# A two-layer transformer with a bidirectional RWKV block: recurrence tiles held by direction, with the two chunks on the two partition halves

## Time and profile before

| | |
|---|---|
| median of 3 runs | 1791.7 us (1791.41 to 1792.92) |
| time of the profiled execution | 1792.95 us |
| its span in the trace | 1791.0 us |
| mean granted TensorE clock | 0.943 of full speed |
| TensorE matmul busy | 1618.8 us (90%) |
| VectorE busy | 764.7 us (43%) |
| ScalarE busy | 376.5 us (21%) |
| DMA | 386.37 MB, mean 216 GB/s |

### The profile page before, as it was taken

How to read it: one execution, slowest core, us unless ns; L and a number is a source line. 1 busy time by engine, 2 the same in 40 slices (tenths; PEclk the granted TensorE clock), 3 DMA queues, 4 the chain that set the end, 5 groups by cost and what they waited for, 6 DMA issues and landing times.

```text
span 1791.0 us, 26168 instructions
## 1 busy us (share of the span) xinstructions
PE 1618.8 (90%) x10862; PEld 1098.8 (61%) x10862; DVE 764.7 (43%) x1562; ACT 376.5 (21%) x959; POOL 2.1 (0%) x6
## 2 busy tenths in 40 slices
PE   8999999999999999999999999999999766666666
PEld 5877878884587787888558778898854101102011
DVE  3476566665538755766555583131422000000001
ACT  4262131110416312211022641111211000000001
POOL 0000000000000000000000000000000000000000
PEclk9999999999999999999999999999999877768777
DMA  9324334535542332544534231111688999999997
GB/s 390 119 72 165 117 134 189 188 149 190 212 152 84 118 143 93 193 177 170 187 144 163 73 142 73 49 50 73 280 322 333 421 420 420 421 421 421 421 421 320
DMA packets 55521, 386.37 MB, mean 216 GB/s; under 512 B 6256, under 2 KB 6768, under 8 KB 10480
## 3 DMA queue, kind: packets, MB, share of 16 engines
q1 hardware_dynamic: 53424, 375.16, 53.2%
q10 hardware_dynamic: 1984, 9.57, 1.4%
HBM read 383.65 MB, written 1.05 MB: 215 GB/s over the span
## 4 chain that ended last, share of the span: by engine, by line
PE 73%; DMA 21%; DVE 2%; ACT 2%; issue 1%; SPq 0%; DVEq 0%; ACTq 0%
PE ps L202 52%; DMA arena<-in_stream 11%; DMA ring<-in_stream 10%; PE ps L2242 3%; PE ps L2223 3%; PE ps L1046 2%; PE ps L1529 2%; PE ps L206 1%; PE ps L1145 1%; PE ps L699 1%; PE ps L1178 1%; PE ps L2383 1%; PE ps L1204 1%; PE ps L1630 0%; PE ps L530 0%
## 5 line engine op out<-in xcount | busy, mean ns | idle before, releaser
L202 PE MATMUL ps<-arena 128*128 128x256 f32 (+4 forms) x2396 | 556.8, 491 | 69.3 <-DMA arena<-in_stream 63.8
L202 PEld LDWEIGHTS ps<-arena 128*128 128x128 f32 (+1 forms) x2396 | 322.0, 171 | 265.9 <-DMA arena<-in_stream 142.4
L202 PE MATMUL ps<-ring,arena 128*128 128x256 f32 (+4 forms) x1132 | 324.8, 512 | 31.8 <-DMA ring<-in_stream 27.2
L202 PE MATMUL ps<-arena,ring 128*128 128x256 f32 (+1 forms) x1228 | 286.0, 380 | 0.0
L202 PEld LDWEIGHTS ps<-ring,arena 128*128 128x128 f32 (+1 forms) x1132 | 175.6, 176 | 156.7 <-issue 69.5
L202 PEld LDWEIGHTS ps<-arena,ring 128*128 128x128 f32 x1228 | 222.3, 192 | 37.4 <-issue 9.6
L2553 PE MATMUL ps<-arena 128*32 128x512 f32 x208 | 140.8, 781 | 0.0
L2760 DVE TENSOR_TENSOR arena<-arena,ps 128x512 f32<-128x512 f32 x8 | 5.5, 688 | 250.6 <-PE ps L2553 250.6
L1093 ACT ACTIVATE arena<-arena,small 128x256 f32<-128x256 f32 x112 | 55.7, 498 | 69.7 <-DVE small L1080 53.2
L2775 DVE TENSOR_TENSOR x<-x,ps 128x512 f32<-128x512 f32 (+1 forms) x18 | 11.3, 628 | 133.7 <-PE ps L2655 133.7
L2553 PE MATMUL ps<-ring,arena 128*32 128x512 f32 x80 | 51.5, 746 | 0.0
(11 more groups left out here) (441 smaller groups left out, 1940.5 us busy)
## 6 DMA issues: line engine op xcount, KB each, us to landing
arena<-in_stream SPq DMA_DIRECT2D x156, 1024.0 KB, 24.8
ring<-in_stream SPq DMA_DIRECT2D x155, 1024.0 KB, 6.4
spare<-in_stream SPq DMA_DIRECT2D x18, 1024.0 KB, 27.7
par<-in_stream SPq DMA_DIRECT2D x9, 1024.0 KB, 26.7
const<-in_stream SPq DMA_DIRECT2D x9, 1024.0 KB, 27.0
par<-in_layer_par ACTq DMA_DIRECT2D x3, 1664.0 KB, 7.4
par<-in_stream SPq DMA_DIRECT2D x8, 512.0 KB, 23.4
const<-in_stream SPq DMA_DIRECT2D x8, 512.0 KB, 24.0
```

The lines of the kernel that those rows point to most:

```text
L202: ins = self.pe.e.matmul(out, lhsT, rhs, start=start, stop=stop)
```

## The change

A tile now belongs to a direction e, and its partition halves are two chunks (token halves of one 128-token block); its 8 slots are the 8 heads. `BETA`, `KAPPA`, `Pb`, `X`, `XT`, `Br`, `Kr` are indexed by e, `Vr` by block. What follows from it:

- first products go over all four quadrants of the array, since the head's half and the chunk's half are now independent, into two banks at a time, one per row half. Their count is the same;
- transposes are full 128x128 ones in transpose mode, 4 per tile (`token_turn`) in place of 16 small matmuls. v is turned in pass 0 only, for both passes;
- a level's P copy, and each of its subtractions, is one instruction over 128x256 in place of two over 128x128; the products keep shape and count;
- the filler of a level is one block of eight ahead of P, in place of four ahead and four behind;
- state: K·V is a product of its own for both steps ahead of the state, copied to X[i] by ScalarE. VectorE adds it to alpha·S. S·rho follows alpha·S and is copied by ScalarE; the rest of y comes in two banks that VectorE adds. VectorE's addition to the state waits until S·rho is computed, and no longer until y is copied.

```diff
+QUADRANTS = [(0, 0), (1, 1), (0, 1), (1, 0)]
...
+def token_turn(p, pe, src, e, blk):
+    bank = opened_bank(p, pe, p.act_tiles)
+    for q in range(PAIRS):
+        ins = pe.e.transpose(bank[:, q * P:(q + 1) * P], src(e, q)[:, blk * P:(blk + 1) * P], p.c("ident"))
+    ins.then_inc(p.act_tiles.full, 1)
...
+def head_order(i):
+    for q in range(PAIRS):
+        for e, par in QUADRANTS:
+            yield e, q, par, rows_of(par), rows_of(half_of(e, i)), 2 * q + par
...
-FILL_EARLY, FILL_PRODUCTS, FILL_FIRST, FILL_LEVEL, FILL_STATE = UNIT_MM, 4, 6, 4, 4
+FILL_EARLY, FILL_PRODUCTS, FILL_FIRST, FILL_LEVEL, FILL_STATE = UNIT_MM, 4, 6, 8, 4
...
+        for e in range(2):
+            blk = block_of(e, m)
+            for left in (beta, kappa):
+                banks = pair_of_banks(p, pe, p.dve_tiles, 4, 2, CH)
+                for q in range(PAIRS):
+                    for par, half in QUADRANTS:
+                        r = rows_of(par)
+                        cols = slice(blk * P + 64 * half, blk * P + 64 * half + 64)
+                        ins = pe.e.matmul(banks[par][rows_of(half), q], left[r, e, q, cols], p.alpha_rho[r, :, e, q, cols])
+                ins.then_inc(p.dve_tiles.full, 2)
+            if m == 0:
+                token_turn(p, pe, lambda e, q: p.shifted[:, 8 + q, :], e, blk)
+            token_turn(p, pe, lambda e, q: beta[:, e, q, :], e, blk)
+            token_turn(p, pe, lambda e, q: kappa[:, e, q, :], e, blk)
             gate_fill_pe(p, pe, w, FILL_PRODUCTS)
...
-            if n:
-                gate_fill_pe(p, pe, w, FILL_LEVEL)
-            for i in range(2 if n else 0):
-                pe.e.wait_ge(p.act_tiles.drained, p.mark[f"P{i}"])
+            for e in range(2 if n else 0):
+                pe.e.wait_ge(p.act_tiles.drained, p.mark[f"P{e}"])
...
+        for i in range(2):
+            bank = shaped(opened_bank(p, pe, p.act_tiles), 8, CH)
+            for e, q, par, r, t, h in head_order(i):
+                ins = pe.e.matmul(bank[t, h, :], p.KAPPA[e][t, h, 0, :], Vr[e][t, h, :])
+            ins.then_inc(p.act_tiles.full, 1)
+            p.mark[f"kv{2 * m + i}"] = p.act_tiles.opened
...
+            banks = pair_of_banks(p, pe, p.dve_tiles, PAIRS, CH)
+            for e, q, par, r, t, h in head_order(i):
+                ins = pe.e.matmul(banks[par][t, q, :], alpha[r, e, q, cols[e]], p.ST[r, e * PAIRS + q, :])
+            ins.then_inc(p.dve_tiles.full, 2)
+            p.mark[f"state_in{c}"] = p.dve_tiles.opened
+            bank = shaped(opened_bank(p, pe, p.act_tiles), 8, CH)
+            for e, q, par, r, t, h in head_order(i):
+                ins = pe.e.matmul(bank[r, e * PAIRS + q, :], p.ST[r, e * PAIRS + q, :], rho[r, e, q, cols[e]])
+            ins.then_inc(p.act_tiles.full, 1)
+            p.mark[f"y{c}"] = p.act_tiles.opened
+            gate_fill_pe(p, pe, w, FILL_STATE)
+            pe.e.wait_ge(p.dve_tiles.drained, p.mark[f"state_in{c}"])
+            bank = shaped(opened_bank(p, pe, p.act_tiles), 8, CH)
+            for e, q, par, r, t, h in head_order(i):
+                ins = pe.e.matmul(bank[t, h, :], p.XT[e][t, h, :], p.Pb[i][t, h, :])
...
+            banks = pair_of_banks(p, pe, p.dve_tiles, PAIRS, CH)
+            for j, e, q, par, r, t, h in head_pairs(i):
+                left, right = ((p.Br[e], p.U), (p.Kr[e], Vr[e]))[j]
+                ins = pe.e.matmul(banks[e][r, q, :], left[t, h, :], right[t, h, :], start=j == 0, stop=j == 1)
+            ins.then_inc(p.dve_tiles.full, 2)
+            banks = pair_of_banks(p, pe, p.dve_tiles, PAIRS, CH)
+            for j, e, q, par, r, t, h in head_pairs(i):
+                left, right = ((p.U, p.BETA[e]), (Vr[e], p.KAPPA[e]))[j]
+                ins = pe.e.matmul(banks[e][r, q, :], left[t, h, :], right[t, h, 1, :], start=j == 0, stop=j == 1)
...
-                for e in range(2):
-                    ins = act.e.activation(level_columns(p.Pb[i][:, 4 * e:4 * e + 4], n, e), level_tile(bank, n, e), ACT.Copy)
...
+                act.e.activation(level_columns(p.Pb[e], n, e), level_tile(bank, n), ACT.Copy).then_inc(p.act_tiles.drained, 1)
+        for i in range(2):
+            copy_out(p.X[i])
...
-            dve.e.wait_ge(p.act_tiles.drained, p.mark[f"y{c}"])
-            e_.tensor_tensor(p.ST, p.ST, bank, ALU.add).then_inc(p.dve_tiles.drained, 1)
+            dve.e.wait_ge(p.act_tiles.drained, p.mark[f"kv{c}"])
+            for par in range(2):
...
+                e_.tensor_tensor(by_parity(p.Pb[i])[:, par], by_parity(p.X[i])[:, par], bank, ALU.add).then_inc(
+                    p.dve_tiles.drained, 1)
+            dve.e.wait_ge(p.act_tiles.full, p.mark[f"y{c}"])
+            for e in range(2):
...
+                e_.tensor_tensor(ST, ST, bank, ALU.add).then_inc(p.dve_tiles.drained, 1)
...
+            dve.e.wait_ge(p.act_tiles.drained, p.mark[f"y{c}"])
+            for e, y in enumerate((p.kd, p.kk)):
...
+                e_.tensor_tensor(y[:, :, cols[e]], y[:, :, cols[e]], bank, ALU.add).then_inc(p.dve_tiles.drained, 1)
```

More of the change, by code:

```diff
@@ L2204, in columns_of, with block_of, rows_of, half_of @@
     return [slice(chunk_of(e, c) * CH, chunk_of(e, c) * CH + CH) for e in range(2)]
-def each_head():
-    for e in range(2):
[L2210 to L2215, removed]
+def block_of(e, m):
+    return m if e == 0 else 1 - m
+def rows_of(half):
+    return slice(64 * half, 64 * half + 64)
+def half_of(e, i):
+    return i if e == 0 else 1 - i
+QUADRANTS = [(0, 0), (1, 1), (0, 1), (1, 0)]
@@ L2217, in head_products, with opened_bank @@
+def opened_bank(p, pe, tiles):
     if tiles.opened >= tiles.size:
         pe.e.wait_ge(tiles.drained, tiles.opened - tiles.size + 1)
[L2219 to L2224, removed]
+    return tiles.open(pe)
+def token_turn(p, pe, src, e, blk):
[3 more added lines that the diff above has]
+    ins.then_inc(p.act_tiles.full, 1)
@@ new lines, in by_parity, with pair_of_banks, head_pairs @@
+def by_parity(ap):
+    return ap.rearrange("p (q two) t -> p two q t", two=2)
+def pair_of_banks(p, pe, tiles, *shape):
+    banks = []
+    for _ in range(2):
+        banks.append(shaped(opened_bank(p, pe, tiles)[:, 0:int(np.prod(shape))], *shape))
+    return banks
+def head_order(i):
+    for q in range(PAIRS):
+        for e, par in QUADRANTS:
+            yield e, q, par, rows_of(par), rows_of(half_of(e, i)), 2 * q + par
+def head_pairs(i):
+    heads = list(head_order(i))
+    for n in range(0, len(heads), 2):
+        for j in range(2):
+            for head in heads[n:n + 2]:
+                yield (j, *head)
@@ L2227, in level_columns, with level_product @@
 def level_columns(ap, n, bit):
     return ap.rearrange("p h (g two s) -> p h g two s", two=2, s=1 << n)[:, :, :, bit, :]
[L2232 to L2242, removed]
+def level_product(p, pe, tiles, n, bit, left, right):
+    bank = shaped(opened_bank(p, pe, tiles)[:, 0:8 * CH // 2], 8, CH // 2)
+    for h in range(HEADS2):
+        for half in range(2):
+            r = rows_of(half)
+            rhs = level_columns(right[:, h:h + 1, :], n, bit)[r, 0]
+            ins = pe.e.matmul(bank[r, h, :].rearrange("p (g s) -> p g s", s=1 << n), left[r, h, :], rhs)
@@ L2243, in level_product, with level_tile @@
     ins.then_inc(tiles.full, 1)
[L2246 to L2251 removed]
+def level_tile(bank, n):
+    return bank[:, 0:8 * CH // 2].rearrange("p (h g s) -> p h g s", h=8, s=1 << n)
+FILL_EARLY, FILL_PRODUCTS, FILL_FIRST, FILL_LEVEL, FILL_STATE = UNIT_MM, 4, 6, 8, 4
 def gate_fill_pe(p, pe, w, n):
@@ L2424, in second_pe @@
[L2424 to L2429, removed]
@@ L2881, in second_act @@
     for m in range(NCH // 2):
[L2882 to L2885, removed]
+        for e in range(2):
+            if m == 0:
+                copy_out(p.Vr[block_of(e, m)])
+            copy_out(p.Br[e])
+            copy_out(p.Kr[e])
             gate_fill_act(p, act, FILL_PRODUCTS)
@@ L3185, in second_dve @@
         for n in range(6):
-            for i in range(2):
+            for e in range(2):
                 if n == 0:
@@ L3189, in second_dve @@
                     bank = shaped(p.dve_tiles.take(dve), 8, CH)
[L3190 to L3194, removed]
+                    e_.tensor_tensor(p.X[e], eye8, bank, ALU.subtract).then_inc(p.dve_tiles.drained, 1)
+                    dve.e.wait_ge(p.sem("level_masked"), 12 * m + e + 1)
@@ L3195, in second_dve @@
+                    e_.tensor_tensor(p.XT[e], eye8, p.Pb[e], ALU.subtract).then_inc(dve.step(), 1)
                     dve.e.wait_ge(dve.steps, dve.n)
-                for dst, other in () if n == 0 else ((p.XT[i], 1),) if n == 5 else ((p.X[i], 0), (p.XT[i], 1)):
+                for dst, bit in () if n == 0 else ((p.XT[e], 1 - e),) if n == 5 else ((p.X[e], e), (p.XT[e], 1 - e)):
                     dve.e.wait_ge(p.dve_tiles.full, p.dve_tiles.turn(dve))
[L3198 to L3205, removed]
+                    part = level_columns(dst, n, bit)
```

(22 more changed lines are left out.)

59 lines of the change are left out of this document (28 added, 31 removed).

## The result

The changed kernel takes 1763.6 us (median of 4 runs, 1761.34 to 1764.22) against 1791.73 us: ratio 0.9842, 95% interval 0.983 to 0.9854. The profiled execution took 1763.91 us, its span 1762.1 us against 1791.0.

A forecast was written before the change was run, and what follows sets the result against it. TensorE's instruction time in the recurrence, plus a few waits, was taken to set the pace, passed on 1:1. Savings of 3.2 + 0.4 + 6.6 + 6.1 + 0.8 = 17.1 us took 1791.7 to 1774.6 us, range 1770 to 1786.

The forecast's parts named there:

- A: Levels of the recurrence: filler in one block saves ten round trips into filler and back, 3.2 us.
- B: First level: a longer filler block hides the wait of the second tile's P for a mask, 0.4 us.
- C: First products on four quadrants: 256 records fall from 56.9 to 31 ns each, 6.6 us.
- D: Transposes: 40 full ones replace the small matmuls, 11.2 us removed, 4.4 added, 0.7 of waits, gain 6.1 us.
- E: State: earlier additions by VectorE remove TensorE's 0.39 us wait between steps, 0.8 us saved in two passes.
- The gap and the clock drop: Recurrence: an unplaced 0.43 us TensorE gap and a half-clock filler block costing 1.26 us; their loss only in the low end.
- no packing gain: First products: four quadrants run no denser than two, so their gain is 0; 1781.2 us, chance 0.14.
- slower: First and state products: quadrants sharing rows or output partitions exclude each other, 27.8 us more, 1809 us; chance 0.06.
- Rival 2: Recurrence: each of four transpose blocks draws a clock drop of 1.26 us; 1779.6 us, chance 0.04.
- Rival 1: Recurrence: longer stretches of small level products draw clock drops, giving back 11.3 us; 1785.9 us, chance 0.18.

The follow-up runs named there:

- The probe: Changed kernel plus nine blocks of 32 unused 64x64 matmuls in the recurrence, to price records by quadrants used (one, two, four) and columns; executed once, 1787.4 us.
- the order by pairs: Changed kernel with the first products ordered two quadrants at a time, same matmuls and banks; 1766.49 us, +3.2.
- the fastest kernel: Changed kernel with four quadrants also in the levels, K·V and XT·Pb, and two early expert units asked for behind weight units 15 and 16; 1750.79 us.

## Why the prediction was wrong

Point by point, by the recurrence's 28.8 us:

- *A and B*, filler blocks: 3.6 forecast, 3.8 measured. Right.
- *C*, first products: 6.6 forecast, 4 x (3.64 - 1.91) = 6.9 measured. Right that four stream at once, at 30 ns a record. That "the floor decides" was wrong here already: 30 is near a quarter of the 109 ns for which 128 columns hold a quadrant, and that this is also near the supposed floor of 29 is luck.
- *D*, transposes: 6.1 forecast. In pass 0 a tile's transposes and filler take 1.93 + 1.73 us for 2.80 + 1.92, in pass 1 they save 1.97 us a tile: 2 x 1.06 + 2 x 1.97 = 6.1. Right, with ScalarE's copy on the path as forecast.
- *E*, the state: 0.8 forecast for the wait between steps, and that was right. **The failed step is its price for the cross-quadrant products**, "from 31 to 29 ns; I leave that to the range (640 records, 1.3 us)". It rested on "below 64 columns something of about 29 ns per record is the floor". A step now takes 0.95 (K·V) + 0.62 + 0.92 + 1.08 + 2.06 (B·U and y) = 5.63 us. Before it took 2.06 (alpha·S and K·V) + 1.08 (XT·Pb) + 4.98 = 8.12 us: 4 x 2.5 = 10.0 us. The probe shows why: what looked like a floor per record is 58 ns per quadrant, 29 with two in turn and 15 with four. Every row of before with 32 and 64 columns had two quadrants in turn, so none could tell a floor of the record from one of the quadrant. I took the first, though the 128-column rows had shown that the quadrant was what filled up.
- The gap and the clock drop: 2.3 us by the profiled execution of the kernel before with the units moved (over whole executions that kernel gained only 0.25 us). I named them only as the low end of the range, as 1.7 us, and as no part of the sum because I couldn't place the gap. The other 0.6 us are the 22 level records behind the gap, which ran at the low clock too (1.24 us where 29 ns each would be 0.64).
- Not forecast: 0.6 us for the bank pair at the boundary of the passes. I had seen the wait and called it nothing.

3.8 + 6.9 + 6.1 + 0.8 + 10.0 + 2.3 - 0.6 = 29.3 us, against 28.8; the 0.5 us over I can't place. The forecast was short by 28.8 - 17.1 = 11.7 us of recurrence. Nearly all of that is the 10.0 of the state and the 2.3 of the gap, less the 0.6 of the boundary.

Of the rivals, no packing gain and slower are refuted by the prices: four quadrants in turn beat two, and none excludes another here. Rival 2, transposes that draw a clock drop, didn't happen: the granted clock was full (1.00) through the recurrence with its 40 transposes. Rival 1 didn't happen either in the changed kernel: the clock was full through the whole recurrence. In the kernel before with blocks of eight the clock did fall, but behind an idle gap; without the gap (units moved) its long stretches kept the full clock.

## What to carry to other kernels

Price small matmuls by the quadrant that they hold, not by the instruction: with 64x64 operands, one that holds its quadrant for 58 ns costs 29 ns with two quadrants in turn and 15 with four, so a layout in which the operands' half and the output's half differ for part of the heads can halve what the products of such a stage cost. In the levels, copies on the path and gaps took back half of the gain that I expected from that. (Each row half wrote its own bank in all of these.) Before calling a common price a floor, look for a row in which the other resource differs. And where TensorE issues dense small matmuls, look in the DMA view for the packets of its instruction queue. In three kernels here one came only behind a pair of 1 MB loads; a gap followed, and then half the clock. With the loads apart, gap and drop went in two, and in the third the gap shrank and the drop went.

## What was unexpected of the hardware

- A record of 32 columns holds its quadrant as long as one of 64: 58 ns both (3.67 us for 63 records each); one of 128 holds it 109 ns.
- Records can start in a free quadrant ahead of earlier ones of the program that wait for theirs (1140.91 against 1140.94 us in the kernel with the prices). That fits the order by pairs, which cost 2.52 us for the first products where 3.6 was expected and 1.91 is the time with four in turn.
- TensorE stood 0.43, 1.77 and 2.92 us in three kernels at the same place, with about 2 MB of weights ahead of a packet of its instruction queue, and went on 2.2 to 2.4 us after the packet; with those loads elsewhere, the gap was 0 in two of them and 0.55 us in the third.
- The granted clock fell to half behind those three gaps, and stayed full through level products without a gap; but it also stayed full behind gaps of 0.55, 1.41 and 0.52 us in the fastest kernel.
